# A hybrid encoder layer: gates and units of the second FFN reordered, residual adds moved, sums of squares on 32-column strips

## The reference

```python
def rmsnorm(x, g):
    return x * rsqrt(mean(x * x, axis=-1) + 1e-6) * g

def swiglu_ffn(x, g, w_gate, w_up, w_down):
    h = rmsnorm(x, g)
    return (silu(h @ w_gate) * (h @ w_up)) @ w_down

x = x + 0.5 * swiglu_ffn_1(x)
x = x + token_mixers(rmsnorm(x))        # band attention and gated delta rule, merged by gates
x = x + cross_attention(x, memory)
x = x + 0.5 * swiglu_ffn_2(x)
y = rmsnorm(x, final_norm)
```

## Time and profile before

| | us |
|---|---|
| median of three runs | 3475.68 (3475.59 to 3482.91) |
| profiled execution | 3480.32 |
| its span | 3478.5 |
| TensorE busy (share) | 3293.7 (95%) |
| VectorE busy | 1288.3 (37%) |
| ScalarE busy | 674.7 (19%) |
| GpSimd busy | 954.7 (27%) |

### The profile page before, as it was taken

One profiled execution on the slowest core, in us unless ns is written; L12 is line 12 of the kernel. 1 busy time (PEld: TensorE's weight loads), 2 busy tenths in 40 slices (PEclk: granted clock), 3 DMA queues, 4 the chain that ended last, 5 costly groups with the idle time before them and its releaser, 6 DMA issues. The chain is left out here.

```text
span 3478.5 us, 50346 instructions
## 1 busy us (share of the span) xinstructions
PE 3293.7 (95%) x19945; PEld 3129.6 (90%) x19945; DVE 1288.3 (37%) x2289; ACT 674.7 (19%) x1302; POOL 954.7 (27%) x436
## 2 busy tenths in 40 slices
PE   6999999999999999988988979999799999999998
PEld 5999999999889888877887879988599999999997
DVE  3232333332445545642442454232225323233324
ACT  5100000000132422433333332123311000000001
POOL 3433333333313123101001023221123333333331
PEclk9999999999999999989999999999899999999999
DMA  5411111111232133112112144024401111111111
GB/s 181 141 37 48 42 42 42 42 36 43 83 109 107 77 119 117 60 69 80 71 38 93 45 157 156 21 96 156 147 31 43 43 48 40 42 40 41 36 48 55
DMA packets 96556, 254.24 MB, mean 73 GB/s; under 512 B 11552, under 2 KB 52640, under 8 KB 93728
## 3 DMA queue, kind: packets, MB, share of 16 engines
q1 hardware_dynamic: 45568, 146.95, 12.3%
q10 hardware_dynamic: 50848, 105.25, 8.4%
HBM read 199.83 MB, written 52.33 MB: 72 GB/s over the span
## 5 line engine op out<-in xcount | busy, mean ns | idle before, releaser
L124 POOL TENSOR_TENSOR w_hi<-w_raw,zero 128x1024 fp32r<-128x1024 f32 x201 | 385.4, 1917 | 2231.3 <-PE psum L155 1320.0
L155 PE MATMUL psum<-x_hi,w_hi 128*128 128x384 f32 x3024 | 598.2, 338 | 51.5 <-DVE x_lo L2136 32.2
L155 PE MATMUL psum<-x_lo,w_hi 128*128 128x384 f32 x3024 | 592.4, 335 | 0.0
L155 PE MATMUL psum<-x_hi,w_lo 128*128 128x384 f32 x3024 | 589.5, 334 | 0.0
L155 PEld LDWEIGHTS psum<-x_hi,w_hi 128*128 128x128 f32 x3024 | 533.6, 189 | 58.1 <-issue 47.6
L155 PEld LDWEIGHTS psum<-x_lo,w_hi 128*128 128x128 f32 x3024 | 533.9, 189 | 0.0
L155 PEld LDWEIGHTS psum<-x_hi,w_lo 128*128 128x128 f32 x3024 | 530.8, 188 | 0.0
L127 POOL TENSOR_TENSOR w_lo<-w_raw,w_hi 128x1024 fp32r<-128x1024 f32 x201 | 500.0, 2488 | 15.8
L394 DVE TENSOR_TENSOR f_hid<-psum,f_gate 128x384 f32<-128x384 f32 x132 | 73.6, 558 | 861.8 <-PE psum L155 859.3
L349 ACT ACTIVATE f_gate<-psum 128x384 f32<-128x384 f32 x132 | 64.7, 493 | 1477.4 <-PE psum L155 1477.4
L155 PE MATMUL psum<-f_h_hi,w_hi 128*128 128x384 f32 x1056 | 269.1, 335 | 0.0
(11 more groups left out here) (276 smaller groups left out, 3354.2 us busy)
## 6 DMA issues: line engine op xcount, KB each, us to landing
w_raw<-units SPq DMA_DIRECT2D x224, 512.0 KB, 3.5
gate_dram<-b_stash ACTq DMA_DIRECT2D x48, 192.0 KB, 1.9
e_gate<-gate_dram ACTq DMA_DIRECT2D x48, 192.0 KB, 2.5
a_kc<-k_cache ACTq DMA_DIRECT2D x4, 2048.0 KB, 7.5
a_vc<-v_cache ACTq DMA_DIRECT2D x4, 2048.0 KB, 13.9
x_sk<-mem_k ACTq DMA_DIRECT2D x8, 1024.0 KB, 8.5
proj_dram<-a_cv ACTq DMA_DIRECT2D x12, 576.0 KB, 2.8
b_pad<-proj_dram SPq DMA_DIRECT2D x12, 576.0 KB, 4.8
```

Of the source, the lines that this page charges most:

```text
L124: pool.tensor_tensor(k.w_hi[s][:, :], k.w_raw[s][:, :], k.zero[:, 0:1].to_broadcast([P, D]), ALU.add)\
L155: mm = pe.matmul(out, wl if part == 2 else wh, (xl if part == 1 else xh)[:, n0:n1], start=(part == 0 and i == 0), stop=(part == 2 and i == ...
```

## The change

1. `product` takes a function `between` and calls it after its first part.
2. `Norm.sums` uses four strips of 32 columns: chunk c goes to strip c % 4, so that each strip holds the sum of two chunks. A new ACT step `gather` copies the bank to the rinv tile, and a new PE step `total` multiplies it with the full matrix of ones; each of 32 equal rows per strip is counted, hence the scale 1 / (32 D) in `root`. `total` is put into the middle of the job after the sum (`between`), or, at an FFN's end, after down job d = 5, and in the memory stage two units later.
3. ffn2's first turn goes third by third over three units (9 jobs); units 3 and 4 wait for 7 and 8 jobs; ACT makes the first two gates, DVE the first hidden row, ahead of `upper` and `lower` of third 2.
4. In residual stages DVE does the add of job 22 ahead of scale chunks 0 to 3 of third 1, then the add of job 23, then chunks 4 to 7 and `lower`.
5. In the memory stage the roots and uppers come one unit later on ACT.

```diff
-def product(pe, out, tiles, n0, n1):
+def product(pe, out, tiles, n0, n1, between=None):
     last = len(tiles) - 1
     for part in range(3):
+        if part == 1 and between:
+            between()
...
-    by_third = [(u, n) for n in range(3) for u in range(2)] + by_unit[6:]
+    by_third = [(u, n) for n in range(3) for u in range(3)] + by_unit[9:]
...
+    def gates_of(i):
+
+        return [(u // 2, n) for u, n in order_of(i) if u % 2 == 0]
...
-            split_units(pool, k, turns, (3, 6, 9, 12, 36, 36), (5, 6, 9, 12, 36, 36), (-1, 0, -2))
+            split_units(pool, k, turns, (3, 6, 9, 12, 36, 36), (7, 8, 9, 12, 36, 36), (-1, 0, -2))
...
-                mm = product(pe, k.ps[g % NPS][:, 0:THIRD], tiles, n * THIRD, (n + 1) * THIRD)
+                mm = product(pe, k.ps[g % NPS][:, 0:THIRD], tiles, n * THIRD, (n + 1) * THIRD,
+                             (lambda: norm.total(pe, 2)) if order is by_third and g == 2 else None)
...
                     if isinstance(i, int) and i == LAST and n >= 1 and d == 4:
                         tail.sums(pe, n - 1)
+                    if isinstance(i, int) and i == LAST and n >= 1 and d == 5:
+                        tail.total(pe, n - 1)
...
         if norm:
             norm.square(act, 2)
+            norm.gather(act, 2)
             norm.root(act, 2)
+            turn(0, gates_of(0)[0:2])
             norm.upper(act, 2)
...
         tail.square(act, 0)
+        tail.gather(act, 0)
         tail.root(act, 0)
         third_added(1)
         tail.square(act, 1)
         if tail.out is None:
             tail.upper(act, 0)
+        tail.gather(act, 1)
         tail.root(act, 1)
...
         if norm:
             norm.scale(dve, 2)
+            hidden(0, 0, 1)
             norm.lower_both(dve, 2)
...
-            mm = pe.matmul(k.ps[4 + n][:, 0:self.width], k.ones[:, :], self.squares[:, c, self.cols(n)],
-                           start=(c == 0), stop=(c == KD - 1))
-        mm.then_inc(s.ntotal.sem, 1)
+            r = 32 * (c % 4)
+            mm = pe.matmul(k.ps[4 + n][r:r + 32, 0:self.width], k.ones[:, 0:32], self.squares[:, c, self.cols(n)],
+                           start=(c < 4), stop=(c >= 4), tile_position=(0, r))
+        mm.then_inc(s.nparts.sem, 1)
+
+    def total(self, pe, n):
+
+        k, s = self.k, self.s
+        pe.wait_ge(s.ngathered.sem, s.ngathered.at(n + 1))
+        pe.matmul(k.ps[4 + n][:, 0:self.width], k.ones[:, :], self.rinv[:, n % 2, :], start=True, stop=True)\
+            .then_inc(s.ntotal.sem, 1)
+
+    def gather(self, act, n):
+
+        k, s = self.k, self.s
+        act.wait_ge(s.nparts.sem, s.nparts.at(n + 1))
+        if n >= 2:
+            act.wait_ge(s.nscaled.sem, s.nscaled.at(2 * (n - 1)))
+        act.activation(self.rinv[:, n % 2, :], k.ps[4 + n][:, 0:self.width], ACT.Copy).then_inc(s.ngathered.sem, 1)
...
-        act.activation(r, k.ps[4 + n][:, 0:self.width], ACT.Ln, bias=k.eps[:, 0:1], scale=1.0 / D)\
+        act.activation(r, k.ps[4 + n][:, 0:self.width], ACT.Ln, bias=k.eps[:, 0:1], scale=1.0 / (32 * D))\
...
-    pe_norm = {3: [lambda pe: norm.sums(pe, 0)], 5: [lambda pe: norm.sums(pe, 1)], 7: [lambda pe: norm.sums(pe, 2)]}
+    pe_norm = {3: [lambda pe: norm.sums(pe, 0)], 5: [lambda pe: norm.total(pe, 0), lambda pe: norm.sums(pe, 1)],
+               7: [lambda pe: norm.total(pe, 1), lambda pe: norm.sums(pe, 2)], 9: [lambda pe: norm.total(pe, 2)]}
...
-            product(pe, k.ps[j % NPS][:, 0:THIRD], tiles, n * THIRD, (n + 1) * THIRD).then_inc(k.dense_done.sem, 1)
+            product(pe, k.ps[j % NPS][:, 0:THIRD], tiles, n * THIRD, (n + 1) * THIRD,
+                    (lambda: tail.total(pe, SUMMED[j - 1])) if j - 1 in SUMMED else None).then_inc(k.dense_done.sem, 1)
...
-            if j in SUMMED:
-                tail.scale(dve, SUMMED[j])
-            if j - 1 in SUMMED:
-                tail.lower_both(dve, SUMMED[j - 1])
+            if SUMMED.get(j) == 0:
+                tail.scale(dve, 0)
+            if SUMMED.get(j - 1) == 0:
+                tail.lower_both(dve, 0)
+            if SUMMED.get(j - 1) == 1:
+                for c in range(4):
+                    tail.scale_chunk(dve, 1, c)
+        for c in range(4, KD):
+            tail.scale_chunk(dve, 1, c)
+        tail.lower_both(dve, 1)
```

More of the change, by code:

```diff
@@ L340, in scalar, with turn @@
     def scalar(act):
-        def turn(i):
+        def turn(i, gates=None):
             at = {un: g for g, un in enumerate(order_of(i))}
-            for c in range(2):
-                for n in range(3):
-                    g = at[2 * c, n]
-                    act.wait_ge(k.dense_done.sem, k.dense_done.at(JOBS * i + (g + 1)))
-                    act.wait_ge(k.gate_used.sem, k.gate_used.at(6 * i + (3 * c + n + 1)))
-                    act.activation(gate[:, n, :], k.ps[g % NPS][:, 0:THIRD], ACT.Silu)\
-                        .then_inc(k.gate_ready.sem, 1)
+            for c, n in gates or gates_of(i):
+                g = at[2 * c, n]
+                act.wait_ge(k.dense_done.sem, k.dense_done.at(JOBS * i + (g + 1)))
+                act.wait_ge(k.gate_used.sem, k.gate_used.at(6 * i + (3 * c + n + 1)))
+                act.activation(gate[:, n, :], k.ps[g % NPS][:, 0:THIRD], ACT.Silu).then_inc(k.gate_ready.sem, 1)
         def third_added(n):
@@ L365, in scalar @@
             bias_rows.store(act)
-        turn(0)
+        turn(0, gates_of(0)[2 if norm else 0:])
         with act.Fori(1, turns) as i:
@@ L380, in scalar, with hidden @@
             tail.upper(act, 0)
+        tail.gather(act, 1)
         tail.root(act, 1)
     def vector(dve):
-        def turn(i):
+        def hidden(i, first, last):
             at = {un: g for g, un in enumerate(order_of(i))}
@@ L387, in turn @@
                 for n in range(3):
+                    if not first <= 3 * c + n < last:
+                        continue
                     g = at[2 * c + 1, n]
@@ L400, in turn @@
                                       ALU.subtract).then_inc(k.h_ready.sem, 1)
+        def turn(i, first=0):
+            hidden(i, first, 6)
             g = 12
@@ L418, in vector @@
             bias_rows.spread(dve)
-        turn(0)
+        turn(0, 1 if norm else 0)
         with dve.Fori(1, LAST) as i:
@@ L533, in tensor @@
             self.sums(pe, n)
+            self.total(pe, n)
     def lower_both(self, dve, n):
@@ L547, in scalar @@
         for n in range(self.nb):
+            self.gather(act, n)
             self.root(act, n)
@@ L590, in tensor @@
         norm.sums(pe, 2)
+        norm.total(pe, 2)
     def scalar(act):
@@ L910, in turn_streams, with job @@
             mm.then_inc(k.ys_turned.sem, 1)
-        def job(i, g, u, n):
+        def job(i, g, u, n, between=None):
             if n == 0:
@@ L918, in job @@
                       xh[:, c, :], xl[:, c, :]) for c in range(KD)]
-            product(pe, k.ps[g % ND][:, 0:THIRD], tiles, n * THIRD, (n + 1) * THIRD)\
+            product(pe, k.ps[g % ND][:, 0:THIRD], tiles, n * THIRD, (n + 1) * THIRD, between)\
                 .then_inc(k.dense_done.sem, 1)
@@ L930, in first_jobs @@
                 for u in range(3):
-                    job(0, 3 * n + u, u, n)
+                    job(0, 3 * n + u, u, n, (lambda: norm.total(pe, 2)) if n == 0 and u == 1 else None)
                     if n == 0 and u == 0:
@@ L2011, in memory_phase @@
     kv, nat = end.kv, end.nat
-    pe_norm = {3: [lambda pe: norm.sums(pe, 0)], 5: [lambda pe: norm.sums(pe, 1)], 7: [lambda pe: norm.sums(pe, 2)]}
+    pe_norm = {3: [lambda pe: norm.sums(pe, 0)], 5: [lambda pe: norm.total(pe, 0), lambda pe: norm.sums(pe, 1)],
+               7: [lambda pe: norm.total(pe, 1), lambda pe: norm.sums(pe, 2)], 9: [lambda pe: norm.total(pe, 2)]}
     act_norm = {0: [lambda act: norm.square(act, 0)], 1: [lambda act: norm.square(act, 1)],
-                2: [lambda act: norm.square(act, 2)], 4: [lambda act: norm.root(act, 0), lambda act: norm.upper(act, 0)],
-                6: [lambda act: norm.root(act, 1), lambda act: norm.upper(act, 1)],
-                8: [lambda act: norm.root(act, 2), lambda act: norm.upper(act, 2)]}
+                2: [lambda act: norm.square(act, 2)], 4: [lambda act: norm.gather(act, 0)],
+                5: [lambda act: norm.root(act, 0), lambda act: norm.upper(act, 0)], 6: [lambda act: norm.gather(act, 1)],
+                7: [lambda act: norm.root(act, 1), lambda act: norm.upper(act, 1)], 8: [lambda act: norm.gather(act, 2)],
+                9: [lambda act: norm.root(act, 2), lambda act: norm.upper(act, 2)]}
     UNITS = 2 * KD
@@ L2290, in scalar @@
             tail.square(act, n)
+            tail.gather(act, n)
             tail.root(act, n)
@@ L2419, in tensor @@
                      for c in range(KD)]
-            product(pe, k.ps[g % 2][:, 0:THIRD], tiles, n * THIRD, (n + 1) * THIRD).then_inc(k.dense_done.sem, 1)
+            product(pe, k.ps[g % 2][:, 0:THIRD], tiles, n * THIRD, (n + 1) * THIRD,
```

(1 more changed line is left out.)

9 lines of the change are left out of this document (4 added, 5 removed).

## The result

The changed kernel takes 3456.82 us (median of four runs, 3451.39 to 3460.05) beside 3477.43 for the kernel before in the same comparison: a ratio of 0.9933, 95% interval 0.9916 to 0.9949. The forecast was 3454, range 3442 to 3468. The profiled execution took 3460.05, the longest of the four; its span is 3458.3 (3478.5 before). So there are 20.2 us to account for, where the prediction had booked 21.7.

The account below looks back on a forecast made before the run. TensorE, busy 95% of the span, bounds the kernel. Terms 1.6 + 6.0 + 4.2 + (4.2 - 1.5) + 7.2 = 21.7 us; against the median of 3475.7 the forecast is 3454 us, range 3442 to 3468.

Parts of the forecast that it names:

- FFN 1 to attention: FFN 1's three sums get shorter, less a stop of 1.2 us and a squares wait of 0.7: gain 6.0 us.
- cross, job 23 to the fifth job: Cross stage: squares come later, but the job waiting for the inverse root starts at 29.6 as before: gain 0.
- wo, sum(0) to job 23: Second residual stage, job 18 to job 23: shorter sums, partly waiting for squares behind scale(0): gain 4.2 us.
- FFN 2, from job 23: FFN 2's start: held scale chunks delay the squares, TensorE stands for 5.4 us: loss 1.5 us.
- end of FFN 2: Last norm: sums 0 and 1 gain 5.3 us, the open last sum 1.9: together 7.2.
- Part 1, the price of a sum: Sums of squares on four strips: a sum with its total costs 2.53 us instead of 5.16, saving 2.63.
- the serial rival: Strip passes run one by one, each sum costing 0.93 us more than before: 3490 us in all; chance 0.05.
- The round trip: Rival: late gathers or strip changes cost TensorE 0.3 to 0.8 us per sum, 4.5 to 12; about 3462; chance 0.15.
- VectorE held by GpSimd: After job 23, VectorE's scale(1) chunks alternate with GpSimd, one per GpSimd instruction: four by 10.3 us, the add at 10.9.
- VectorE is not held: Rival: scale chunks run at free speed; FFN 2 gains another 6 us, cross 2.5; 3445 us; chance 0.20.
- The clock: Rival: stretches at the lower granted clock fall elsewhere, about 3 us either way; no chance of its own given.
- The reordering does nothing: Rival, already in the forecast: the add of job 23 comes early, yet the squares wait on upper(1).

Follow-up runs that it names:

- change_again: The changed kernel unaltered, run again on the same chip as its variants; 3452.29 us, ratio to before 0.9931.
- rinv_in_psum: Against the changed kernel, ScalarE's Exp writes the inverse root into PSUM and VectorE's scale chunks read it there; 3438.40 us, 3440.62 in the later comparison.
- squares_first: Against chunks_first, ScalarE makes the squares of third 2 in the residual stage, ahead of the second half of upper(1); 3444.24 us, ratio to before 0.9894.
- reorder_only: The changed kernel without its strips: full-array sums, no gather or total, all new orders kept; 3480.71 us beside 3480.63, ratio to before 1.0000.
- chunks_first: Against the changed kernel, scale chunks 0 to 2 of third 1 go ahead of the add of job 22, chunk 3 behind it; 3448.96 us, ratio to before 0.9908.

## Why the prediction was right

The forecast missed the median by 3 us, and most steps came as written. That it is so near is in part luck: of the terms below five came out better than booked, by 3.5 us together, and four worse, by 5.0. The terms in the profiled execution, each a difference between distances of starts on PE ("FFN 1 to attention" runs from FFN 1's sum(0) to mix's). The last column has the same distances in the trace of change_again, the same code in another execution, 8.9 us shorter:

| term | booked | measured | change_again |
|---|---|---|---|
| memory stage | 1.6 | 1.9 | 3.0 |
| FFN 1, a stretch at the lower clock | 0 | -1.5 | -0.1 |
| FFN 1 to attention | 6.0 | 7.5 | 11.8 |
| mix, sum(0) to job 23 | 4.2 | 4.8 | 4.8 |
| cross, job 23 to the fifth job | 0 | 0.5 | 0.5 |
| cross, behind it (clock) | 0 | -1.6 | 0.8 |
| wo, sum(0) to job 23 | 4.2 | 4.8 | 4.8 |
| FFN 2, from job 23 | -1.5 | -2.3 | -2.6 |
| end of FFN 2 | 7.2 | 6.1 | 6.1 |
| sum | 21.7 | 20.2 | 29.1 |

The five terms around the stage changes (mix, cross to the fifth job, wo, FFN 2 and its end) repeat within 0.3 us. The other four differ by 1.1 to 4.3 us between two executions of the same code, so a miss of 1 or 2 us there tells nothing of the change.

**Part 1, the price of a sum.** Booked 1.6 + 0.93 = 2.53, a saving of 2.63. Measured around 2573.42: 1.43 for the sum and 0.19 more in the product groups on its two sides (1.48 and 1.49 for 1.39), so 1.62; 0.35 for the total and 0.30 behind it, 0.65 for a booked 0.93. That is 2.27, a saving of 2.89; the total was the mis-sized term, and it is why mix and wo gained 0.6 us more than booked and the two hidden sums at FFN 2's end 0.3 each. The passes do lie side by side: the serial rival is out. The prediction took a drain at each change of the tiling mode from the Trainium skill (TensorEngine Tiling (Array Packing), Key Properties) and put it at 2 x 0.16 = 0.32 us a sum on top of the booked 1.6. The sum cost 1.62, so nothing of that size came on top. What the rows leave room for is the 0.19 beside the sum and 0.21 in it (1.43 for four rounds of 0.304); they can't say whether any of it is a drain.

**The round trip.** It leaked little. The total waits 0.78 us in FFN 1 behind upper(0), where 1.2 was booked, and 0.61 in the last norm; the other two waits of the 3.7 us in front of L506 (1.01 and 1.32) lie in the memory stage, where TensorE is not the limit. That rival's 4.5 to 12 us did not come.

**FFN 1 to attention.** The total of third 1 started at 936.45 after a wait of 0.78, and the sum of third 2 stands in two halves, 0.52 us apart where 0.7 was booked:

```profile
936.45 0.91 PE L506 MATMUL psum<-n_rinv,ones 128*128 128x384 f32 x2 [0.78 <-ACT n_rinv L515]
...
954.91 0.85 PE L498 MATMUL psum<-n_squares,ones 128*32 128x384 f32 x8 [0.83 <-ACT n_squares L488]
956.28 0.85 PE L498 MATMUL psum<-n_squares,ones 128*32 128x384 f32 x8 [0.52 <-ACT n_squares L488]
```

From FFN 1's sum(0) to attention's sum(2) the change gains 4.8 us, booked 4.1, and around sum(2) another 2.4, booked 1.9; change_again has 4.8 and 2.4 too.

**VectorE held by GpSimd.** This was read from one stretch, and VectorE's steps held within half a microsecond. Predicted from job 23: four chunks by 10.3, add 23 at 10.9, the sum's end at 21.6 after a stop of 5.4. Measured: four chunks by 10.0 (2605.6), add 23's end at 10.5 (2606.1), the sum's end at 21.7 (2617.27), a stop of 4.75. The sum's end agrees by luck: its squares came 0.65 us sooner than booked, and the low clock made the sum 1.4 us longer. In cross the sum was to end at 18.1 and ends at 17.7. The fifth job there, which the earlier trace rows shows without a releaser, was booked at 29.6 and starts at 29.1, behind a wait of 2.13 us for its low parts. "VectorE is not held" (0.20) is ruled out by 2743 ns against 616. Its prices were near: with the hold gone (rinv_in_psum) C is 6.7 us shorter and cross up to the fifth job 3.0, where that rival had 6 and 2.5. What I did not price is that the stop lowers the clock: without the 2.6 us for that, FFN 2 would stand at about +0.3 in place of -2.3, where -1.5 was booked.

**The end of FFN 2** was too high, and there the step that failed is the last sum: booked 1.9, measured 0.3 (sum(2) to the end of the span 17.08 us before, 16.80 after). The other two saved 2.9 and 3.0. PE's rows of the last norm, and two stretches of it with the grant:

```profile
3441.47 0.85 PE L498 MATMUL psum<-n_squares,ones 128*32 128x384 f32 x8 [2.17 <-ACT n_squares L488]
3442.85 1.50 PE L498 MATMUL psum<-n_squares,ones 128*32 128x384 f32 x8 [0.52 <-ACT n_squares L488]
3444.97 1.65 PE L506 MATMUL psum<-n_rinv,ones 128*128 128x384 f32 x2 [0.61 <-ACT n_rinv L515]
```

```profile
3441.00:3443.00 2.00, 1.00 (x12) 0.31 (x16) 2.00 (x5) 1.80 (x2) 0.00 (x0) 0.88 0.00 0
3443.00:3446.00 3.00, 2.39 (x10) 0.55 (x6) 1.14 (x3) 0.49 (x1) 0.00 (x0) 0.50 0.30 110
```

The grant falls to 0.5 behind the idle time of 2.17 us, and the second half of the sum and the total take nearly twice as long; before, it stayed at 1.00 from 3461 to 3466, through the same steps. squares_first has the same code here, the same waits, and a grant of 1.00:

```profile
3428.36 0.85 PE L497 MATMUL psum<-n_squares,ones 128*32 128x384 f32 x8 [0.52 <-ACT n_squares L487]
3429.82 0.91 PE L505 MATMUL psum<-n_rinv,ones 128*128 128x384 f32 x2 [0.61 <-ACT n_rinv L514]
```

Its sum(2) to the end takes 15.40 us, 1.7 less than before. So the steps behind the booked 1.9 were nearly right, and the clock took 1.4 us back ((1.50 - 0.85) + (1.65 - 0.91)). Why the grant falls here in one execution and not in another was not tried.

**The clock** was allowed 3 us either way. In the profiled execution it cost about 3 in FFN 1 and cross (a grant of 0.50 from 125 to 128 behind a wait of 2.32 for a gate, and from 2272 to 2275 behind one of 2.13) and 2.6 in FFN 2. In change_again the same two waits of 2.32 and 2.13 have a grant of 1.00 behind them, so those 3 us belong to the execution and not to the change; the fall behind the stop in FFN 2 comes back in it. The mean grant of the profiled execution was 0.979 against 0.983 before; the other three of the comparison had 0.981 to 0.983.

**The reordering does nothing** was put as part of the forecast, and reorder_only (1.0000) bears that out. Why it does nothing was right only in part: not because the squares wait on upper(1) alone, but because scale(1) and GpSimd alternate; squares_first (on top of chunks_first) removes the wait on upper(1), rinv_in_psum the alternation, and each ends the stop before the sum.

## What to carry to other kernels

Where VectorE reads two operands from SBUF beside GpSimd's elementwise work, count one VectorE instruction for each GpSimd instruction, and see which of the two TensorE waits for; one operand in PSUM, or an order that keeps the two apart, gives it back. A reordering should be priced with that collision in and with it out, because it can be worth nothing in the one and 0.2 to 0.3% in the other. A step on the path that gets shorter than its feeder turns into a wait, and a wait of some us can lower TensorE's clock for the work behind it.

## What the runs showed of the hardware that was not expected

The alternation works on both engines: short VectorE chunks are stretched from 0.54 to 2.3 us while GpSimd's instructions lengthen by only 0.2 to 0.3, but VectorE's low steps of 1.7 us stretch GpSimd's instructions from 1.9 and 2.4 to 3.41 and 3.75 and are stretched to 3.5 themselves (6.99 us for two). Reading the inverse root from PSUM did not lengthen the chunks at all (median 609 ns for 614). Two matmuls in a row on one strip cost nothing as long as the other strips' matmuls stand behind them in the queue, ready to run. And where the two engines start 0.01 us apart, the same code can end either way: 2.41 or 0.23 us for one VectorE instruction of 64 columns.
